# Attention scores of two heads in the two row halves of TensorE, units in pairs, without padded keys

## The reference, cut to what matters

```
# first block, mixer "nsa": 16 heads, 2 key groups of 8 heads; two branches of
# the same shape (o_slc over all visible key blocks, o_win a causal window of 512)
s = einsum('bcghd,bkgd->bcghk', q_rope, k) * DH ** -0.5      # 64-wide contraction
p = masked_softmax(s, mask);  o = einsum('bcghk,bkgd->bcghd', p, v)
o = gates[..., 0:1] * o_cmp + gates[..., 1:2] * o_slc + gates[..., 2:3] * o_win
# first block, mixer "dilated": 16 heads with keys of their own; heads 0-5 a band of
# 128 keys, heads 6-10 every 4th key, heads 11-15 every 16th
# second block, "win": 8 heads, 2 key groups of 4, a window of 128 keys, a sink per head
e = exp(s - m);  p = e / (sum(e) + exp(sink - m))
```

## Time and profile before

| | us |
|---|---|
| median of 3 runs (2568.28 to 2576.03) | 2572.22 |
| the profiled execution, its time | 2572.68 |
| its span, first to last instruction | 2570.9 |
| nsa stage, first pad to last finish | 294.3 to 509.7 |
| dil stage | 782.3 to 855.2 |
| win stage | 1110.3 to 1148.0 |

### The profile page before, as it was taken

How to read it: one execution, slowest core, us unless ns; L and a number is a source line. 1 busy time by engine, 2 the same in 40 slices (tenths; PEclk the granted TensorE clock), 3 DMA queues, 4 the chain that set the end, 5 groups by cost and what they waited for, 6 DMA issues and landing times. The chain is left out here.

```text
span 2570.9 us, 31761 instructions
## 1 busy us (share of the span) xinstructions
PE 2295.3 (89%) x11763; PEld 1961.8 (76%) x11763; DVE 1595.2 (62%) x2898; ACT 910.4 (35%) x1484; POOL 1320.2 (51%) x699
## 2 busy tenths in 40 slices
PE   2699699988998678885799999999999799999998
PEld 1588578766787555664588998999999688777787
DVE  6321588645504637454407999999997366666765
ACT  1212355322225413242223333345555333333332
POOL 0333001134541321411243788886665699999996
PEclk7799799899999788897899999999999899999999
DMA  6322164422220011200123787889998799999996
GB/s 227 131 93 97 38 226 164 163 82 68 86 89 4 17 66 41 76 32 25 57 82 120 243 290 264 287 294 364 348 349 304 282 342 341 346 348 342 340 339 250
DMA packets 164185, 492.22 MB, mean 191 GB/s; under 512 B 15040, under 2 KB 64320, under 8 KB 162624
## 3 DMA queue, kind: packets, MB, share of 16 engines
q1 hardware_dynamic: 107584, 305.62, 34.6%
q0 software_dynamic: 36864, 134.23, 14.3%
q10 hardware_dynamic: 19584, 50.34, 5.1%
HBM read 437.70 MB, written 52.43 MB: 191 GB/s over the span
## 5 line engine op out<-in xcount | busy, mean ns | idle before, releaser
L1799 POOL TENSOR_TENSOR t_split<-t_raw,t_split 128x1024 fp32r<-128x1024 f32 x256 | 625.4, 2444 | 154.1 <-ACT t_split L1726 150.2
L237 PE MATMUL ps<-h_hi,w_split 128*128 128x512 f32 x1760 | 579.9, 406 | 49.9 <-DVE h_lo L360 30.6
L215 POOL TENSOR_TENSOR w_split<-ring,w_split 128x1024 fp32r<-128x1024 f32 x113 | 272.8, 2418 | 576.5 <-ACT w_split L207 576.3
L1692 PE MATMUL ps<-t_split,w_split 128*128 128x512 f32 x2304 | 532.0, 392 | 17.7 <-DVE w_split L1968 13.7
L1658 PE MATMUL ps<-h_hi,t_split 128*128 128x384 f32 x2048 | 536.5, 338 | 7.7 <-POOL t_split L1799 4.6
L1692 PEld LDWEIGHTS ps<-t_split,w_split 128*128 128x128 f32 x2304 | 431.3, 188 | 118.2 <-DVE w_split L1968 14.1
L237 PEld LDWEIGHTS ps<-h_hi,w_split 128*128 128x128 f32 x1760 | 337.5, 192 | 141.6 <-issue 42.5
L1726 ACT ACTIVATE t_split<-t_raw 128x1024 fp32r<-128x1024 f32 x256 | 270.3, 1056 | 371.0 <-DMA t_raw<-v_table 201.0
L1658 PEld LDWEIGHTS ps<-h_hi,t_split 128*128 128x128 f32 x2048 | 372.8, 189 | 10.3 <-POOL t_split L1799 6.9
L237 PE MATMUL ps<-h_lo,w_split 128*128 128x512 f32 x880 | 349.1, 397 | 0.0
L1658 PE MATMUL ps<-h_lo,t_split 128*128 128x384 f32 x1024 | 343.4, 335 | 0.0
(11 more groups left out here) (269 smaller groups left out, 3013.2 us busy)
## 6 DMA issues: line engine op xcount, KB each, us to landing
ring<-w_stream SPq DMA_DIRECT2D x219, 512.0 KB, 3.7
t_raw<-u_table SPq DMA_DIRECT2D x128, 512.0 KB, 4.7
t_raw<-v_table SPq DMA_DIRECT2D x128, 512.0 KB, 4.8
gelu_scratch<-e_gel ACTq DMA_DIRECT2D x128, 192.0 KB, 4.8
gates_scratch<-arena ACTq DMA_DIRECT2D x8, 3072.0 KB, 13.4
arena<-gelu_scratch SPq DMA_DIRECT2D x32, 768.0 KB, 5.5
arena<-gates_scratch SPq DMA_DIRECT2D x32, 768.0 KB, 8.8
xT<-x_in SPq DMA_DIRECT2D x2, 1024.0 KB, 11.2
```

Of the source, the lines that this page charges most:

```text
L215: pool.tensor_tensor(w_split[:, i % RS, 1, :], ring[:, n % R, :], w_split[:, i % RS, 0, :].bitcast(F32), ALU.subtract).then_inc(lo_done, 1)
L237: mm = pe.matmul(ps[:, bank, :], w[:, a, k * P:(k + 1) * P], src[b][:, k, :], start=(k + a + b == 0), stop=(k == KD - 1 and a == 1))
L1692: mm = pe.matmul(ps[:, 2 * i + half, :], w_split[:, b % 2, w, at:at + P], t_split[:, m % RAWS, v, half * 512:(half + 1) * 512], start=(n + ...
L1799: pool.tensor_tensor(t_split[:, m % RAWS, 1, :], t_raw[:, m % RAWS, :], t_split[:, m % RAWS, 0, :].bitcast(F32), ALU.subtract).then_inc(t_ ...
```

## The change

`attention` loses `pads`. Scores are taken from the unpadded keys with 64-partition operands: head A's query and key rows 0 to 63, head B's rows 64 to 127, so that two successive units use the two row halves of TensorE. Units are ordered so that the two halves alternate: in nsa head u of group 0, then head u of group 1; in win 0, 4, 1, 5, ...; in dil the order stays (2u, 2u + 1). A unit gets a sixth field, its place among the 8 of its group of outputs, which `column()` and the output slot use. PE's loop goes in steps of two: both scores, then both units of transposes, both of weighted sums, then the fillers. LT goes from 3 to 4, LP from 5 to 6; the buffer counts (SB 3, PB 4, TB 3) stay. The nsa finish reads its gates, and POOL its sums, in the new order of heads with views of the same size.

```
-            LT, LP = 3, 5
+            LT, LP = 4, 6
...
+            def column(n):
+                c = n - n % 8 + units[n][5]
+                return slice(c, c + 1)
...
-                pad_zero.wait(pe, 2 * len(pads))
-                pad_dve.wait(pe, len(pads))
-                pad_act.wait(pe, len(pads))
-                for n in range(N + LP):
-                    if n < N:
-                        if n >= SB:
-                            neg_done.wait(pe, n - SB + 1)
-                        pe.matmul(ps[:, n % SB, 0:len(vb) * P], q, k, start=True, stop=True).then_inc(s_done.sem, 1)
-                    if LT <= n < N + LT:
...
+                for n in range(0, N + LP, 2):
+                    for j in (n, n + 1):
+                        if j < N:
+                            scores(j)
+                    for j in (n, n + 1):
+                        if LT <= j < N + LT:
+                            turned(j - LT)
+                    for j in (n, n + 1):
+                        if LP <= j < N + LP:
+                            weighted(j - LP)
+                    for j in (n, n + 1):
+                        if pe_filler and j < N:
+                            pe_filler(pe, j)
...
-                for dst, src in pads:
-                    act.activation(dst[DH:P, 1], src[DH:P], ACT.Copy).then_inc(pad_act.sem, 1)
...
-                for dst, src in pads:
-                    dve.tensor_copy(dst[0:DH, 0], src[0:DH]).then_inc(pad_dve.sem, 1)
...
-                for dst, _ in pads:
-                    pool.memset(dst[DH:P, 0], 0.0).then_inc(pad_zero.sem, 1)
-                    pool.memset(dst[0:DH, 1], 0.0).then_inc(pad_zero.sem, 1)
...
+        def half_rows(g):
+            return slice(g * DH, (g + 1) * DH)
...
-                for h in range(NH):
-                    g = h // 8
-                    nsa_units.append((qr[:, 2 + h % 8, tile_tokens(i)], ks_pad[:, g, ku, 0:(i + 1) * P],
...
+                for u in range(8):
+                    for g in range(2):
+                        nsa_units.append((qr[half_rows(g), 2 + u, tile_tokens(i)],
+                                          qr[half_rows(g), ku, 0:(i + 1) * P],
...
-                    dil_units.append((qd[:, u, class_tokens(i)], keys[:, u, class_tokens(i)], mask,
-                                      [vd[:, i, cols]], BIG))
+                    dil_units.append((qd[rows, u, class_tokens(i)], kd[rows, u, class_tokens(i)], mask,
+                                      [vd[:, i, cols]], BIG, h % 8))
...
-            for h in range(NQ2):
+            for h in (0, 4, 1, 5, 2, 6, 3, 7):
```

More of the change, by code:

```diff
@@ L745, in _, with attention @@
                             ins.then_inc(c_out, 1)
-        def attention(tag, block, units, work, finish, finish_pool=None, pe_filler=None, dve_filler=None, ask=0,
-                      pads=()):
-            LT, LP = 3, 5
+        def attention(tag, block, units, work, finish, finish_pool=None, pe_filler=None, dve_filler=None, ask=0):
+            LT, LP = 4, 6
             CY = 4
@@ new lines, in scores, with turned @@
+                def scores(n):
+                    q, k, _, vb, _, _ = units[n]
+                    if n >= SB:
+                        neg_done.wait(pe, n - SB + 1)
+                    pe.matmul(ps[:, n % SB, 0:len(vb) * P], q, k, start=True, stop=True).then_inc(s_done.sem, 1)
+                def turned(m):
+                    exp_done.wait(pe, m + 1)
+                    if m >= 2:
+                        wait_copied(pe, m - 2)
+                    for b in range(len(units[m][3])):
+                        mm = pe.transpose(ps[:, 3 + m % 2, b * P:(b + 1) * P],
+                                          prob[:, m % PB, b * P:(b + 1) * P], ident)
+                    mm.then_inc(t_done.sem, 1)
@@ new lines, in weighted @@
+                def weighted(m):
+                    wait_copied(pe, m)
+                    if m % 8 == 0 and m >= 16:
+                        o_read.wait(pe, m // 8 - 1)
+                    vb, slot = units[m][3], units[m][5]
+                    for b, v in enumerate(vb):
+                        mm = pe.matmul(ps[:, 5 + (m // 8) % 2, slot * DH:(slot + 1) * DH],
+                                       prt[:, m % TB, b * P:(b + 1) * P], v,
+                                       start=(b == 0), stop=(b == len(vb) - 1))
+                    mm.then_inc(pv_done.sem, 1)
@@ L894, in nsa_finish @@
             dve.wait_ge(dve_step, v)
-            v = note("dve", dve.tensor_tensor(r, r, gate[:, i, 24 * half + 1 + branch:24 * half + 24:3], ALU.mult))
+            gated = gate[:, i, :].rearrange("p (g u b) -> p b g u", g=2, b=3)[:, 1 + branch, :, 4 * half:4 * half + 4]
+            by_pair = r.rearrange("p (g u) -> p g u", g=2)
+            v = note("dve", dve.tensor_tensor(by_pair, by_pair, gated, ALU.mult))
             dve.wait_ge(dve_step, v)
@@ L907, in nsa_finish_pool @@
                     pool.wait_ge(added, g - 7)
-                dst = ot[:, i, half * 512:(half + 1) * 512]
-                pool.tensor_tensor(dst, dst, gtmp[:, g % 2, :], ALU.add).then_inc(added, 1)
+                dst = ot[:, i, :].rearrange("p (g n) -> p g n", g=2)[:, :, half * 256:(half + 1) * 256]
+                pool.tensor_tensor(dst, dst, gtmp[:, g % 2, :].rearrange("p (g n) -> p g n", g=2),
+                                   ALU.add).then_inc(added, 1)
         ada_sum = place("ada_sum", HR_AT + 4 * T, [2, PIECE])
@@ L1111, in build @@
             for h in range(NH):
-                u, keys = h // 2, kd_pad[:, h % 2]
+                u, rows = h // 2, half_rows(h % 2)
                 cols = slice(h * DH, (h + 1) * DH)
@@ L1134, in build @@
             dnmax, dden = attention("dil", block, dil_units, 20480, plain_finish(
-                lambda g: od[:, g // 2, (g % 2) * 512:(g % 2 + 1) * 512].rearrange("p (h d) -> p h d", d=DH)),
-                pads=[(kd_pad[:, :, u:u + 2, :], kd[:, u:u + 2, :]) for u in range(0, KD, 2)])
+                lambda g: od[:, g // 2, (g % 2) * 512:(g % 2 + 1) * 512].rearrange("p (h d) -> p h d", d=DH)))
         lse = area(20480, TT, NH)
@@ L1392, in build @@
         with phase() as block:
-            wnmax, wden = attention("win", block, win_units, 18440, win_finish, pads=[(k_pad, qr9[:, 4:5, :])])
+            wnmax, wden = attention("win", block, win_units, 18440, win_finish)
         at11, m11 = area(2048, 4, T), area(4096, 8, T)
```

55 lines of the change are left out of this document (15 added, 40 removed).

## The result

The changed kernel takes 2613.4 us (median of 4, 2591.4 to 2618.4), the kernel before on the same chip 2573.7 us. The ratio is 1.0141 with a 95% interval of 1.0081 to 1.0201: slower by 1.4%, where 2551 was forecast and 2572 was the top of the range. The profiled execution has a span of 2611.3 us.

The account below looks back on a forecast made before the run. PE was taken to bound dil and win, PE and DVE in turn nsa; 13.5 (padding) + 5.9 (overlap less changes) - 2 (schedule) + 4 (nsa's end) = 21.4 us off 2572.7, so 2551 us, range 2528 to 2572.

Parts of the forecast that it names:

- Term 1: Start of nsa, dil and win: the wait for padding before the first score is removed whole, 13.5 us won.
- Term 2: Paired scores on PE: the two row halves overlap, saving one pass of four, 31.5 us; bounds 0 and 63.
- Term 3: PE's 224 changes between half-row scores and full-row work cost 0.10 us each, 22.4 us; upper bound 0.30 each, 67 us.
- drain rival: Every change between half-row and full-row work on PE costs 0.30 us; 2590 us, slower; chance 0.12.
- Term 4: PE's pair loop with SB = TB = 3: waits on buffers lose 2 us in nsa, nothing in dil's strided units; bounds 0 to 4.
- the copy behind the weighted sum: Odd unit's copy waits for weighted(n - 6) of the same iteration; as a rival, nsa 13.4 us more, 2565 us, chance 0.08.
- Term 5: End of nsa: shorter PE idle, so part of the drain runs at full clock, 4 us won (0 to 10); nothing for dil, win.

Follow-up runs that it names:

- e7: Kernel before with padding off the path: nsa's pads written in the block before, dil's units waiting only for their own pad; 2566.5 us, ratio 0.9976.
- e6: Kernel before plus stretches of 512-column fp32 matmuls (full rows, one half, halves in turn, mixed) before win's first score; single run, clock 1.00 in every stretch.
- e9: Kernel before plus five PE-only stretches of 24 attention-like units without waits, each after 12 full-row matmuls; run once, 0.14 us a change.
- e2: Changed kernel's pair schedule with the padded full-row keys of before put back; 2574.2 us, ratio 1.0004.
- e12: e2 with TB = 4, one more buffer, freeing the odd unit's copy from its own iteration's weighted sum; 2579.5 us, ratio 1.0016.
- e4: Changed kernel plus one full-row matmul of 256 columns per pair that nobody reads; 2583.8 us, ratio 1.0031.
- e1: Changed kernel's half-row scores without pads, but PE's loop as before: one unit at a time, LT 3, LP 5; 2850.7 us, ratio 1.1078.
- e3: Changed kernel with both units of a pair in the same row half, so they can't run side by side; 2806.1 us, ratio 1.0909.
- S5: Stretch of e9: 256-column score and four sums, all on rows 0 to 63, no change of rows; clock 0.55, staying at 0.50 after about 6 us.
- S4: Stretch of e9: full-row 256-column score and four full-row sums, no transposes; clock stayed at 1.00, a unit 1.32 us.
- S2: Stretch of e9: scores on rows 0 to 63 and 64 to 127 in turn, transposes and sums full-row; clock 1.00, a unit 1.38 us.

## Why the prediction was wrong

**Term 1 (padding, 13.5 us): right as a time.** First scores stand at the opening of their blocks. What it is worth in the whole was measured for 9.7 us of it only, in e7, and was about 6 there. (In the earlier trace rows the 2.18 us before line 207 are ACT's idle before its first work, not a time after an idle as the prediction has it; nothing hangs on it.)

**Term 2 (one pass of four saved): the halves do run side by side, but wholly, and so two passes of four are saved.** That is the term's own upper bound, 63 us, of which 31.5 was booked. With both changes paid (0.10 us for the one outside the interval), a pair saves 0.19 us for nb = 2, where 0.25 - 0.20 was booked, 0.21 for strided pairs (0.30 - 0.20 booked) and about 0.6 for nb = 4 (0.46 - 0.20). The halves don't keep the program order A1 A2 B1 B2: e6 shows lower and upper passes starting together even right after full-row work. TensorE: Matmul & The Clock Gate in the Trainium skill, Part 3, says that matmuls start and end in strict program order; e6's trace doesn't bear that out for the passes of two row halves.

**Term 3 (0.10 us a change): too small.** e9 has 0.14 beside short passes, e6 0.20 beside 512-column ones; 224 changes at these prices are 31 to 45 us where 22.4 were booked. The drain rival's 0.30 did not occur. TensorEngine Tiling (Array Packing) in the Trainium skill, Key Properties, has a change of tiling mode drain the array; a cost of 0.14 to 0.20 us agrees with that in kind. Terms 2 and 3 were both too small and partly cancel.

**Term 4 (pair schedule, 2 us lost): the sum was about right by luck, the places were not.** e2 keeps the padding and loses nothing overall: nsa 8 us longer, win 3 and dil 1.4 shorter. The mechanism that was named, the copy behind the weighted sum, was tested in e12 and is not it.

**Term 5 is the step that failed.** It ended: "In dil and win less idle stands before the first score, but the thin start of the pipeline remains; I take nothing for the clock there." Every PE price in terms 2 to 4 was taken from rows at 1.00 and carried over to work of another kind. The clock of dil and win went to 0.52 instead. No rival had it, and the last line of the prediction, which named the cost of a change as the only thing that could make it wrong, looked in the wrong place. How much it was can be estimated from e4, which has the same half-row pairs at a full clock: dil 70 - 14 = 56 us against 85, win 41 - 7 = 34 against 55 (e4's win lies between 1119 and 1160, at 0.96, with 16 added matmuls). That is 50 us in these two stages, so with the clock held there for free the changed kernel would stand near 2563 us, 10 below before. By the same estimate nsa would be up to 20 us shorter (233 - 64 x 0.43 = 205 against 226). The forecast of 2551 lies between 2543 and 2563: apart from the clock its sum was about right, though by errors in terms 2 and 3 that partly cancel. Of the forecast's 4 us for nsa's end only a part came: the chunk ran at the full clock, 2.16 us for 3.57, but after its wait of 2.68 us the rest of the pipeline drained at 0.50.

```profile
503.83 2.16 PE L277 MATMUL ps<-cst,ada_sum 128*128 128x1 f32 x16 [2.68 <-DVE ada_sum L269]
...
506.00:512.00 6.00, 6.00 (x30) 6.00 (x31) 0.00 (x0) 1.20 (x3) 0.00 (x0) 0.50 0.10 37
```

What is shown: the low clock is the cause (e4 adds work and is faster), in dil and win it comes with the half rows and not with the schedule (e2, e1, e3), and half rows can bring it about by themselves (S5 against S4, one run). What stays open is what decides. S2, a unit much like e1's, kept 1.00 without waits, though e1's PE hardly waited either (busy 421 of 425 us in nsa); e1 began nsa at 0.50 and dil with the thin start of the pipeline, and S2 came behind 12 full-row matmuls at 1.00. No run starts S2 at 0.50 or puts waits into it.

## What to carry to other kernels

Before packing small contractions into row halves, look at the granted clock of the stage and ask what the packed work leaves for the array to do. Here the packed scores took 0.63 us for 0.92 and the stage still grew from 73 to 85 us, because PE got half its clock, and a PE that the profile shows busy 15.00 of 15 us gave no hint of it. And read the clock in short windows, in stages that the change seems to leave alone too: nsa's came and went by 4 to 10 us from one full-row kernel to the next. Zero padding costs a pass nothing on PE (20.8 us for 24 matmuls on all rows or on half of them); what it cost here was a wait, and taking 9.7 us of it off the path gave about 6 without touching the matmuls.

## What the runs showed of the hardware

- A gapless PE can be at a clock of 0.50: e1's nsa was busy 421 of 425 us at 0.50. In e9, 24 units on 64 rows fell from 1.00 to 0.50 within about 6 us where the same 24 units on 128 rows stayed at 1.00, yet long 512-column passes on 64 rows stayed at 1.00 for 20.8 us (e6).
- fp32 passes of the two row halves run wholly side by side: 0.43 us for a lower and an upper pass of 512 columns, the length of one.
- Going between 64-row and 128-row work costs 0.14 to 0.20 us a change (e9, e6).
- Side by side or not also matters to the clock: the same half-row passes with the same changes had 0.83 in nsa when the two halves overlapped (the changed kernel) and 0.53 when they couldn't (e3).
- Full rows can lose it too: in nsa of e2 it fell to 0.50 four times between 310 and 490 us, each time 1.5 to 3 us after PE began 16 one-column passes.
- Adding 112 full-row matmuls that nobody reads, 48 us of PE work, made the changed kernel some 30 us faster (e4).
